# Seven block products in place of eight for 14 pairs of up-projection tiles, with the root mean square moved behind the down projection

## The reference

```
def rmsnorm(x, g):
    xf = x.astype(F32)
    y = xf * lax.rsqrt(jnp.mean(xf * xf, axis=-1, keepdims=True) + EPS)
    return (y * g.astype(F32)).astype(x.dtype)
...
        u = rmsnorm(h, w['mlp_norm'][l]) @ w['w_up'][l]
        h = h + jnp.square(jax.nn.relu(u)) @ w['w_down'][l]
    return rmsnorm(h, w['final_norm']), jnp.stack(ret_states), new_ckr
```

## Time and profile before

| | |
|---|---|
| Time, median of 3 runs | 1550.87 us (1549.12 to 1551.77) |
| The profiled execution: its time, its span | 1550.3 us, 1548.2 us |
| TensorE matmul busy, instructions | 1517.9 us (98%), 11519 |
| VectorE busy | 808.0 us (52%) |
| ScalarE busy | 575.7 us (37%) |
| GpSimd busy | 49.5 us (3%) |
| DMA | 149.74 MB, mean 97 GB/s |

### The profile page before, as it was taken

How to read it: one execution, slowest core, us unless ns; L and a number is a source line. 1 busy time by engine, 2 the same in 40 slices (tenths; PEclk the granted TensorE clock), 3 DMA queues, 4 the chain that set the end, 5 groups by cost and what they waited for, 6 DMA issues and landing times.

```text
span 1548.2 us, 28948 instructions
## 1 busy us (share of the span) xinstructions
PE 1517.9 (98%) x11519; PEld 1419.1 (92%) x11519; DVE 808.0 (52%) x1282; ACT 575.7 (37%) x904; POOL 49.5 (3%) x74
## 2 busy tenths in 40 slices
PE   7999999999999999999998999999999999999998
PEld 6999999899999999999998667667999999999998
DVE  4867777665434334344577566655553343343444
ACT  5633333233313223133443275554443132231333
POOL 1110000020000000000001000000000000000000
PEclk9999999999999999999999999999999999999999
DMA  8473323342222332222334415523222232222221
GB/s 247 119 202 81 82 82 85 107 134 82 83 82 82 89 89 82 83 82 82 83 82 121 122 49 146 149 70 102 70 81 83 83 93 83 82 83 82 82 83 61
DMA packets 231407, 149.74 MB, mean 97 GB/s; under 512 B 11297, under 2 KB 225074, under 8 KB 231282
## 3 DMA queue, kind: packets, MB, share of 16 engines
q1 hardware_dynamic: 217666, 122.81, 28.0%
q0 software_dynamic: 5968, 20.18, 4.4%
q10 hardware_dynamic: 7648, 4.98, 1.1%
HBM read 140.26 MB, written 7.68 MB: 96 GB/s over the span
## 4 chain that ended last, share of the span: by engine, by line
PE 88%; DVE 7%; ACT 2%; issue 1%; DMA 1%; ACTq 0%; DVEq 0%
PE ps L641 70%; PE ps L1253 3%; PE ps L1127 3%; PE ps L1280 2%; DVE wl L1876 1%; PE ps L1223 1%; PE ps L1186 1%; PE ps L1187 1%; DVE t L2292 1%; PE ps L1106 1%; DVE onorm L2077 1%; PE ps L1109 1%; DMA xsrow<-in_x_sample 1%; ACT memE L1455 1%; DVE gn L2071 0%
## 5 line engine op out<-in xcount | busy, mean ns | idle before, releaser
L1371 ACT ACTIVATE wh<-raw 128x1024 fp32r<-128x1024 f32 (+1 forms) x194 | 201.2, 1037 | 600.7 <-PE ps L641 591.5
L641 PE MATMUL ps<-xh,wh 128*128 128x288 f32 x1542 | 336.4, 300 | 3.2 <-DVE wl L1876 1.7
L641 PE MATMUL ps<-xh,wl 128*128 128x288 f32 x1542 | 328.6, 295 | 0.0
L641 PE MATMUL ps<-xl,wh 128*128 128x288 f32 x1542 | 328.1, 294 | 0.0
L641 PE MATMUL ps<-mh,wh 128*128 128x288 f32 (+1 forms) x1408 | 318.8, 295 | 2.4 <-DVE t L2292 1.7
L641 PE MATMUL ps<-mh,wl 128*128 128x288 f32 (+1 forms) x1408 | 317.1, 294 | 0.0
L641 PE MATMUL ps<-ml,wh 128*128 128x288 f32 (+1 forms) x1408 | 316.9, 294 | 0.0
L1876 DVE TENSOR_TENSOR wl<-raw,wh 128x1024 fp32r<-128x1024 f32 (+1 forms) x194 | 231.8, 1195 | 70.0 <-ACT wh L1371 67.9
L641 PEld LDWEIGHTS ps<-xh,wh 128*128 128x128 f32 x1542 | 247.4, 189 | 9.9 <-DVE wl L1876 5.1
L641 PEld LDWEIGHTS ps<-xh,wl 128*128 128x128 f32 x1542 | 247.3, 188 | 0.0
L641 PEld LDWEIGHTS ps<-xl,wh 128*128 128x128 f32 x1542 | 247.2, 188 | 0.0
(11 more groups left out here) (337 smaller groups left out, 1313.1 us busy)
## 6 DMA issues: line engine op xcount, KB each, us to landing
raw<-in_w_up SPq DMA_DIRECT2D x64, 512.0 KB, 4.0
raw<-in_w_down SPq DMA_DIRECT2D x64, 512.0 KB, 4.0
pages<-in_cache_mla SPq DMA_DIRECT2D x128, 160.0 KB, 2.2
raw<-in_a_w_in SPq DMA_DIRECT2D x24, 512.0 KB, 4.0
memkc<-in_cache_mem_k POOLq DMA_DIRECT2D x16, 256.0 KB, 4.5
memvc<-in_cache_mem_v POOLq DMA_DIRECT2D x16, 256.0 KB, 5.6
raw<-in_a_w_out SPq DMA_DIRECT2D x8, 512.0 KB, 4.1
raw<-in_b_w_out SPq DMA_DIRECT2D x8, 512.0 KB, 4.3
```

Source lines behind the costliest of these rows:

```text
L641: last = mm(ps[:, 2 * (m % 2) + c, 0:n], w[:, kk, :], x(kk, col, n), start=(kk == 0 and nth == 0), stop=(kk == final and nth == 2))
L1371: do(f(split(m)[0][:, 0:k, :], raw[:, m % NRAW, 0:k, :], ACT.Copy), C[whi_ready])
```

## The change

In seven of the sixteen pairs of up tiles of each layer (KINDS: S is such a pair, P a plain one; each S follows a P), the product of a 2 x 2 block matrix of weights (two k-halves, two tiles) with a 2 x 2 block matrix of inputs (two k-halves, two halves of the rows) is made by seven block products with sums of blocks, in place of eight. Each product is 4 k-tiles x 3 part products = 12 matmuls of 288 columns. The sums of input blocks are made once a layer, in fp32 by GpSimd (input_sums), and split by ScalarE and VectorE (sum_head, sum_tail). VectorE makes the four sums of weight blocks (weight_sum), and each of the seven weight blocks is split by itself (pair_head on ScalarE, pair_tail on VectorE). VectorE combines the products from PSUM in t12 (pair_take), ScalarE then has relu, square and rounding for the whole pair (hidden).

relu no longer multiplies by rstd. rstd is squared once, and each down tile is multiplied by it before it is added to the residual. The first two down tiles of each group are interleaved on TensorE: k-tiles 0 to 5 of both, then 6 and 7 of both. The loops over groups of ScalarE and VectorE are written out. GpSimd's loads for layer 1 are issued after the last up tile of layer 0. Some semaphores of the memory attention are shared between the layers.

```diff
+KH = KD // 2
+KINDS = ('PPPS', 'PSPS', 'PSPS', 'PSPS')
+PRODUCTS = 7
...
 # GpSimd
+            def input_sums(layer):
+                x0 = (8, 24)[layer]
+                for n, (k, c) in enumerate(((0, 0), (0, 1), (1, 1), (1, 0))):
+                    if n % 2 == 0:
+                        pool.wait_ge(x_lo, x0 + KH * k + KH)
+                    do(pool.tensor_tensor(block_x[n][:, :, :], half_block(xh, k, c).bitcast(F32), half_block(xl, k, c).bitcast(F32), ALU.add))
...
+            input_sums(0)
+            pool.wait_ge(acc_ready, M_MLP[0] + LAP * (NGROUP - 1) + GROUP)
...
 # TensorE
+                    product(0, m, n, X, x, block_of(0, 0))
+                    if follows:
+                        pe.wait_ge(p_taken, n)
+                    else:
+                        pe.wait_ge(acc_free, freed(m))
+                    product(1, m, n, Y, x, block_of(1, 0))
...
+                    pe.wait_ge(p_lo, split_by(layer, NPAIR * layer))
+                    product(2, m, n, Z, sums, sum_of(2))
+                    product(3, m, n, Z + 1, sums, sum_of(0))
+                    product(4, m, n, Y + 1, sums, sum_of(1))
...
+                    product(5, m, n, W + 1, sums, sum_of(3))
+                    product(6, m, n, W, x, block_of(1, 1))
...
-                    for j in range(KD - 1):
-                        dense(m0 + base + GROUP + j, tiles(mh), tiles(ml),
-                              ready=(h_lo, lambda kk: h0 + GROUP * g + kk + 1) if j == 0 else None)
+                    for part in (range(KD - 2), range(KD - 2, KD)):
+                        for j in range(2):
+                            dense(m0 + base + GROUP + j, tiles(mh), tiles(ml), part=part, ready=(h_lo, lambda kk: h0 + GROUP * g + 2 * (kk // 2) + 2))
+                    for j in range(2, KD - 1):
+                        dense(m0 + base + GROUP + j, tiles(mh), tiles(ml))
...
 # ScalarE
+                        act.wait_ge(acc_free, freed(m0 + base + j + 1))
                         do(f(t2[:, :], t1[:, :], ACT.Square))
                         do(f(mh[:, j, :], t2[:, :], ACT.Copy), C[h_hi])
+                        if g == 0 and j == 2 * FIRST - 2:
+                            for n in range(4):
+                                sum_head(n)
+                        if is_pair(g, q + 1):
+                            for p in (SECOND_PART if j % 2 else FIRST_PART):
+                                pair_head(p, g, q + 1)
...
 # VectorE
+                do(tt(rstd[:, :], rstd[:, :], rstd[:, :], ALU.mult))
...
+                def first_tails(g, q):
+                    pair_tail(0, g, q)
+                    weight_sum(1, g, q)
+                    weight_sum(3, g, q)
+                    pair_tail(1, g, q)
+
+                def second_tails(g, q):
+                    pair_tail(2, g, q)
+                    weight_sum(2, g, q)
+                    weight_sum(4, g, q)
+                    pair_tail(3, g, q)
+                    pair_tail(4, g, q)
...
-                        dve.wait_ge(acc_ready, at(m + 1, i))
-                        do(stt(halves(t1[:, :]), acc(m), 0.0, halves(rstd[:, :]), ALU.max, ALU.mult), C[acc_free])
-                        w_tail(m + 2, i)
-                        dve.wait_ge(h_hi, at(h0 + base // 2 + j + 1, i, GROUP))
+                        dve.wait_ge(acc_ready, m + 1)
+                        do(ts(halves(t1[:, :]), acc(m), 0.0, None, ALU.max), C[acc_free])
+                        if not is_pair(g, q + 1):
+                            w_tail(m + 2)
+                        dve.wait_ge(h_hi, h0 + GROUP * g + j + 1)
                         do(tt(ml[:, j, :], t2[:, :], mh[:, j, :].bitcast(F32), ALU.subtract), C[h_lo])
+                        if g == 0 and j == 2 * FIRST - 2:
+                            for n in range(4):
+                                sum_tail(n)
+                        if is_pair(g, q + 1):
+                            (second_tails if j % 2 else first_tails)(g, q + 1)
...
-                        add_residual(m, j, i)
+                        dve.wait_ge(acc_ready, m + 1)
+                        do(tt(halves(t1[:, :]), halves(rstd[:, :]), acc(m), ALU.mult))
+                        do(tt(res[:, j, :], res[:, j, :], t1[:, :], ALU.add), C[acc_free])
```

More of the change, by code:

```diff
@@ L1210, in unit_values @@
                     return
[L1211 removed]
+                pe.wait_ge(u_pt, MEM_UNITS + q + 1)
                 if q:
@@ L1634, in out_and_mlp, with sum_head @@
                     head(xh[:, j, :], res[:, j, :], G_MLP + 8 * layer + j, C[x_hi])
[L1635 removed]
+                m0, h0 = M_MLP[layer], GROUP * NGROUP * layer
                 root((3, 7)[layer], D, rstd[:, :])
[L1638 to L1642 removed]
+                def sum_head(n):
+                    act.wait_ge(p_input, 8 * layer + 5 + n)
+                    do(f(sum_h[:, n, :, :], sum_f[n][:, :, :], ACT.Copy), C[p_hi])
@@ new lines, in out_and_mlp, with group @@
+                FIRST_PART, SECOND_PART = (0, 1), (2, 3, 4)
+                def group(g):
+                    base, last = LAP * g, g == NGROUP - 1
+                    for j in range(GROUP):
+                        q = j // 2
+                        if is_pair(g, q):
+                            if j % 2 == 0:
+                                pair_take(g, q)
+                            continue
+                        if j % 2 == 0 and is_pair(g, q - 1):
+                            hidden(g, q - 1)
+                        if not is_pair(g, q + 1):
+                            w_head(m0 + base + j + 2)
+                        act.wait_ge(acc_free, freed(m0 + base + j + 1))
@@ L1661, in group @@
                                 do(f(ytmp[:, j, :], res[:, j, :], ACT.Copy, scale=gain[:, G_FIN + j:G_FIN + j + 1]), C[y_ready])
-                        if m + 2 < M_END:
-                            w_head(m + 2, i)
-                with act.Fori(0, NGROUP - 1) as i:
-                    for c, lap in ((own, GROUP), (C[whi_ready], LAP), (C[h_hi], GROUP)):
-                        c.enter(i, lap)
-                    group(0, i)
-                for c in (own, C[whi_ready], C[h_hi]):
-                    c.leave(NGROUP - 1)
-                group(LAP * (NGROUP - 1))
+                        if last or j < KD - 2 or not is_pair(g + 1, 0):
+                            if m + 2 < M_END:
+                                w_head(m + 2)
+                        else:
+                            for p in (SECOND_PART if j % 2 else FIRST_PART):
+                                pair_head(p, g + 1, 0)
+                for g in range(NGROUP):
+                    group(g)
             out_and_mlp(0, G_KVN)
@@ L2259, in group @@
                                 part = slice(HALF * c, HALF * c + HALF)
-                                do(tt(res[:, j, part], res[:, j, part], ps[:, 2 * (m % 2) + c, 0:HALF], ALU.add), C[y_res])
+                                do(tt(t1[:, part], rstd[:, part], ps[:, 2 * (m % 2) + c, 0:HALF], ALU.mult))
+                                do(tt(res[:, j, part], res[:, j, part], t1[:, part], ALU.add), C[y_res])
                                 dve.wait_ge(y_sq, c + 1)
@@ L2269, in group @@
                                 tail(xl[:, j, :], res[:, j, :], g_next + j, xh[:, j, :], C[x_lo])
-                        if m + 2 < M_END:
-                            w_tail(m + 2, i)
-                with dve.Fori(0, NGROUP - 1) as i:
-                    for c, lap in ((C[wlo_ready], LAP), (C[acc_free], LAP), (C[h_lo], GROUP)):
-                        c.enter(i, lap)
-                    group(0, i)
-                for c in (C[wlo_ready], C[acc_free], C[h_lo]):
-                    c.leave(NGROUP - 1)
-                group(LAP * (NGROUP - 1))
+                        if last or j < KD - 2 or not is_pair(g + 1, 0):
+                            if m + 2 < M_END:
+                                w_tail(m + 2)
+                        else:
+                            (second_tails if j % 2 else first_tails)(g + 1, 0)
+                for g in range(NGROUP):
+                    group(g)
             out_and_mlp(0, G_KVN)
```

282 lines of the change are left out of this document (240 added, 42 removed).

## The result

The changed kernel took 1596.96 us (median of 4 runs, 1595.09 to 1598.19) beside 1551.32 us for the kernel before on the same chip (4 runs, 1549.12 to 1552.92): a ratio of 1.0294, 95% interval 1.0276 to 1.0312. The profiled execution took 1595.09 us with a span of 1593.3, that is 44.8 us more than the profiled execution before. The forecast was +31.2, with 1573 to 1592 us as its range and 1562 to 1600 with its rivals.

A forecast was written before the change was run, and what follows sets the result against it. TensorE, busy 98% of the span, was taken as the bound. Terms -21.2 + 22.0 + 11.2 + 18.5 + 0.2 + 0.5 = +31.2 on 1550.3 gave 1582 us, range 1573 to 1592 (1562 to 1600 with rivals).

The forecast's parts named there:

- the rival on the clock: After each of four long TensorE stalls a tile runs at 0.24 us a matmul: +10 to +21, 1592 to 1603; chance 0.15.
- my own signs: Wrong if the named MLP waits are absent, products' pace leaves 131 to 133 ns, or the clock shows below 1.00.
- Matmuls: In 14 product pairs, 84 matmuls at 0.1325 us replace 96 at 0.1317: -1.51 us each, -21.2 us.
- Wait in the pairs: Products 2 and 3 wait for late weight splits, 0.98 + 0.59 us in each of 14 pairs: +22.0 us.
- Input sums: Four input-sum splits ahead of each layer's first product pair delay its products, 5.6 us above the ordinary wait: +11.2 us.
- Down tiles: Third down tile waits for its weights' split, 1.65 us in six groups and 4.3 in two last groups: +18.5 us.
- GpSimd's sums: GpSimd's eight input sums a layer are ready before use, so cost 0, with 0 to +10 for the range.
- Squaring of rstd: One more VectorE product of 0.76 us ahead of the first relu, before the third up tile: 0.1 a layer, +0.2 us.
- The end: At the very end the second half's multiply (0.454 + 0.03) is on the chain: +0.5 us.
- faster: VectorE and ScalarE reach the pairs' and d2's splits at least 3 us sooner, all stalls go: 1530 us; chance 0.05.
- only the down tiles stall: The product pairs do not stall because the gaps overlap: 1548 us, no change; chance 0.04.
- only the pairs stall: The third down tile's split is ready, so only product pairs wait: 1563 us; chance 0.09.

The follow-up runs named there:

- The first experiment: Changed kernel with the splits of products 2 and 3 and weight sums 2 and 4 ahead of VectorE's wait for the last plain tile's rounding: 1573.51 us, 1.0144.
- the third experiment: Changed kernel with GpSimd's last six input sums held back until the third up tile's weights are split: 1590.75 us, 1.0264.
- the kernel with only the down tiles: Changed kernel without any block product or GpSimd input sums; interleaved down tiles, moved root mean square and written-out groups remain: 1572.66 us, 1.0152.
- the four moves: Changed kernel with earlier product splits, input-sum splits over two tiles, staggered down tiles, and d2's split ahead of the squares in last groups: 1544.64 us, 0.9973.
- the six pairs: Four edits of VectorE, ScalarE and TensorE order kept, but six product pairs a layer and GpSimd's sums held until group 0's down tiles: 1547.56 us, 0.9988.
- fifth experiments: Changed kernel with TensorE's down-tile order staggered: d0 blocks 0 to 5, d1 0 and 1, d0 6 and 7, d1 2 to 7: 1582.15 us, 1.0205.
- The additions alone: Kernel before plus six unused GpSimd additions (128x1152) in layer 0, from when the first up-projection's inputs stand: 1552.0 us, 1.0013.

## Why the prediction came out as it did

The direction and the mechanism were right: matmuls saved are paid back more than twice by waits for VectorE, at the three places named. The size was off, +44.8 by the profiled executions for a forecast of +31.2: 1597 us lies above the forecast's own range (1573 to 1592) and inside the wider one, in the 1592 to 1603 of the rival on the clock. That it fits the rival is in part luck: the clock carries under half of the excess, and as much comes from a term that I had put at nothing. By my own signs the forecast was wrong in one point: the clock in the MLPs shows 0.99.

- **Matmuls, forecast -21.2.** 11351 are left, as forecast. The pace was read slightly too fast: a product's matmuls start 0.133 us apart (489.90 to 491.23 is ten), not 0.1325, and by the spacing of their starts the plain ones take 0.1319, not 0.1317. This makes the saving about 1.4 us smaller.
- **Wait in the pairs, +22.0.** Product 3 in the pair shown starts to 0.01 us where the working put it. The first experiment took 0.0150 off the ratio, 23.3 us. Right.
- **Input sums, +11.2.** Product 3 of the first pair was due at 11.1 and came at 18.36 in layer 1 (forecast 18.3), 0.3 later in layer 0. Right.
- **Down tiles, +18.5.** 1.57 and 4.30 measured for 1.65 and 4.3, 0.5 us less in all. The kernel with only these was 23.2 above before for 19.2 of terms and half clock behind. Right in the waits.
- **GpSimd's sums, taken at 0.** This step failed. I priced them by when their result is wanted, and they are ready in time; what they cost is VectorE's time beside them. VectorE's subtraction takes 2.75 us instead of 1.23, and the third tile is 3.1 us late in both layers: 6.2 us, 6.0 beyond the 0.2 forecast for this place. The prediction weighed a rule of the Trainium skill, "SBUF — State Buffer", section "SBUF: two separate sides" (an operation of VectorE with two inputs in SBUF and one of GpSimd exclude each other for a whole instruction), and left it out of the sum. The trace agrees with the rule: the stretched operations are those with two SBUF inputs, and the one reading PSUM kept its 0.76 us. With the estimate of 2.5 us for an addition, from the Trainium skill, "GPSIMD Engine Reference", section 3.1, it would have made the sum 5 us higher; measured additions took 2.67 us and, against VectorE's operations, up to 3.51.
- **Squaring of rstd, +0.2.** It takes 0.76 us where no addition runs beside it (in the third experiment and in the kernel with only the down tiles), but here it is itself stretched to 2.66; its 1.9 us more is part of the 6.2 above.
- **The end, +0.5.** From the end of the last window to the end of the span it is 12.3 us, 11.8 before. Right.
- **The clock, a rival at 0.15.** It did fall, behind all six long waits of the profiled execution. The rival charged 48 matmuls at 0.108 us extra, and 10 to 15 were. Those of the first pairs cost nothing, as I read it: products 2 and 3 there wait for VectorE anyway, so slow matmuls only shorten that wait. Behind the other four waits it is 57 matmuls in all: 57 x 0.108, +6.2. At the 0.240 us from start to start that the earlier trace rows show, the rival's price for one matmul was right; its number of them was too high.
- **The first matmuls behind a wait.** Two matmuls at 434.50 took 0.37 us instead of 0.264. I had nothing for it; behind the 14 waits ahead of product 3 and the 6 short ones ahead of d2 it is some 0.1 us each, +2.

1.4 + 0.3 - 0.5 + 6.0 + 6.2 + 2 is 15.4, of an excess of 46.2 - 30.7 = 15.5 us in the MLPs (30.7 is the sum without the 0.5 at the end). The terms are not known to 0.1 us, so that they meet so closely is chance. Outside the MLPs the two profiles differ by 1.1 us in the other sense. The third tile's waits and the clock carry 12.2 of it. That the clock fell in these places was seen in the profiles; its part of the time is worked out and has no experiment of its own. The spread of the executions of one kernel goes the same way (those with the lower mean clock mostly took longer, as shown for the four moves and the six pairs). Why the clock fell behind a wait of 3.1 us in one kernel and not behind the same wait in another (376.11 above) stays open.

The rivals "faster", "only the down tiles stall" and "only the pairs stall" are out: both kinds of wait are there, and each was removed by itself (the first and fifth experiments).

## What to carry to other kernels

When TensorE is full and another engine prepares its operands just in time, price a saving of matmuls against the slack of that engine at each place, by the time from the last tile's end to the next operand's readiness, not by its busy share: VectorE at 61% cost more here than the products saved, and moving work ahead of a wait on the same engine gave the pairs' 23 us back. An engine that "only adds in the background" is to be priced by what it does to the others' operations beside it; give it one operation a tile, where the other engine has idle time. Count for each long wait of TensorE (2.0 to 4.3 us here) 1 to 3 us for the matmuls at half clock behind it too (8 to 24 at 0.108), unless a later wait hides that.

## What the hardware showed beyond that

- An addition by GpSimd of 128x1152 fp32 and VectorE's operations with two inputs in SBUF hold each other up whole: 0.76 becomes 2.3 to 3.1 us and 1.23 becomes 2.1 to 3.6, where most of the operation's own length falls beside an addition, and the addition itself goes from 2.67 to as much as 3.56 (in "The additions alone"). VectorE's operations with one input in PSUM and one in SBUF kept their 0.76 us beside the same additions, and the reciprocal of rstd, with one input in SBUF, its 3.75.
- In the profiles of nine of the kernels, 35 waits of TensorE in the MLPs lasted 2.0 to 4.3 us, and behind 31 of them a run of 8 to 24 matmuls at the clock's lower level followed (all six in the changed kernel); behind four of about 3.1 us none did. Behind waits of 1.8 us and less none followed. The run often began later than the restart, by 0.5 to 1.4 us in 13 of the 31 cases (in the one shown under "The clock" by 1.2 us).
